# Reordering the two sums of the first down-projection slot in a fused diffusion backbone

## The chip, the cores and the metric

One core of one Trainium2 chip. The metric is the device time of one execution in microseconds. The engines named below are TensorE (PE; its weight loads are PEld), VectorE (DVE), ScalarE (ACT), GpSimd (POOL) and SyncE (SP, which issues most DMAs). Work of different engines is ordered by semaphores alone.

## What is computed

A two-layer backbone over 256 context and 256 latent tokens with 1024 features. Each layer is FFN, token mixer, FFN. The mixer of layer 0 is a state-space layer (S5) with a gated output (glu), that of layer 1 a gated DeltaNet. So there are four FFNs, f0 to f3:

```python
def swiglu(h, w13, w2):
    a, b = jnp.split(h @ w13, 2, axis=-1)
    return (jax.nn.silu(a) * b) @ w2
# D_MODEL 1024, D_FF 2816
h = ada_norm(x, norm_g[i, 0], mx[:, 0], mx[:, 1])
x = x + 0.5 * mx[:, 2] * swiglu(h, ffn_w13[i, 0], ffn_w2[i, 0])
```

The vectors `mx` (shift, scale, gate) come from the products of a conditioning vector with `mod_w`. f0, f1 and f2 are computed for all 512 tokens, f3 for the 256 latent tokens only. All is float32.

## The kernel before

**Numbers.** Every operand of a large product is split into a high part in the reduced format fp32r and the rest (low part). One tile product is three matmuls: high x high, low x high, high x low (`mm3`, L220: L223, L224 and L225). The stationary operand is a 128x128 weight tile, the moving one 512 columns of tokens (256 in f3).

**Stages.** An FFN has 22 inner tiles (2816 / 128), worked in three parts, `PARTS`, of n = 8, 8 and 6 inner tiles; "f1p2" is part 2 of FFN 1. A part has an up phase of n slots (one slot makes one inner tile of both products `a` and `b`, L242) and a down phase of four slots. A down slot takes one weight block and makes two output tiles: q = 0 in PSUM bank 4 and q = 1 in bank 5, each a sum over the part's n inner tiles. Slots alternate between two weight buffers, s = 0 and 1; a loop step i has both.

**Hidden tiles.** After an up slot ACT takes the SiLU (L636), DVE multiplies (gate, L665), POOL makes the high copy `hidh` (L722) and the low part `hidl` (L724), and increments `hid_ready`. The last of these is made while the first down slot runs. There TensorE goes through q = 0 tile by tile, waits for the last two tiles at k = n-2 and n-1 (L601), and then goes through q = 1.

**Waits of a down slot on TensorE.** `weights_in(pe, 0, ...)` and `weights_in(pe, 1, ...)` wait for the halves of the weight block, the second at the eighth tile product (`HALF // P`, L598). `x_ready[q]` (L596) says that DVE has used the bank's last sum. After q = 0 `acc_even` is incremented (L605), and in some slots `mods_turn` follows (L607, eight small transposing matmuls of L774, with which computed mod vectors are handed to DVE). After q = 1 `blk_done` is incremented (L609). `mods_step` and, in f0, `tables_pe` (L612, L613) follow the slot.

**DVE in a down slot** (`update`, L669), in fixed order: `mods_take` where `mods_turn` was issued; wait for `acc_even`; first update of `x` (`add_to_x`, L707, two instructions for 512 columns, then `x_ready[0]`); in f0 `tables_first_dve` (L680: tables for the state-space layer, bx at L1115 to L1117 and cx at L1151 to L1153, in slots set by a table); in f1p2 `mods_dve` (L682, four reductions of L786) in both slots with s = 0; wait for `blk_done`; second update (`x_ready[1]`). Between two `update`s stand the `split_lo` (L278) of the next weight block, which frees `raw` for SP's next load, and which itself follows ACT's `split_hi` (L272). The split of the weights for the first down slot stands ahead of the last gate.

**Loops.** `loop` (L527) runs a body as a hardware loop (`Fori`) or written out. On TensorE the down phases of f0 are written out (g is a number there), those of f1, f2 and f3 are loops of two steps.

Of the kernel before, what the change touches and what calls it, by code (L numbers as in the profile page):

```python
# [21 lines left out]
KT = D // P  # L22
# [71 lines left out]
def mods_where(f, p):  # L94

    g = MODS_IN.get((f, p))
    return g is not None and g >= PE_GROUPS
# [10 lines left out]
X_BEFORE = [sum(X_UPDATES[:m]) for m in range(len(NORMS) + 1)]  # L108
# [5 lines left out]
def pieces_before(m, of=("ffn", "s5", "gdn")):  # L114

    return sum(p for p, (_, _, _, k) in zip(PIECES[:m], NORMS[:m]) if k in of)
# [9 lines left out]
def program(nc, A, out):  # L126

    ctx = ExitStack()
    with ctx:
# [3 lines left out]
        def pair(name):  # L133
            return [sem(f"{name}{i}") for i in range(2)]
# [21 lines left out]
        early = ExitStack()  # L156
# [58 lines left out]
        x_ready = pair("x_ready")  # L215
# [4 lines left out]
        def mm3(pe, dst, slot, c, xh, xl, first, last):  # L220

            w_h, w_l = whi[:, slot, c:c + P], wlo[:, slot, c:c + P]
            pe.matmul(dst, w_h, xh, start=first, stop=False)  # L223
            pe.matmul(dst, w_h, xl, start=False, stop=False)  # L224
            return pe.matmul(dst, w_l, xh, start=False, stop=last)  # L225
# [10 lines left out]
        def mm3_pair_low_last(pe, dsts, slot, cs, xh, xl, low, first, last):  # L236

            for of, moving in ((whi, xh), (wlo, xh), (whi, xl)):
                if moving is xl and low:
                    pe.wait_ge(norm_done, low)  # L240
                for dst, c in zip(dsts, cs):
                    ended = pe.matmul(dst, of[:, slot, c:c + P], moving, start=first and of is whi and moving is xh, stop=last and moving is xl)  # L242
            return ended
# [19 lines left out]
        def weights_in(pe, half, s, use):  # L263

            pe.wait_ge(wlo_ready[half][s], 1 + use + 1)
# [38 lines left out]
        def halves(c0):  # L304
            return [w for w in range(2) if w * CTX >= c0]
# [221 lines left out]
        def loop(eng, n, written_out, body, first=0):  # L527

            if written_out:
                for i in range(first, n):  # L530
                    body(i)
            else:
                with eng.Fori(first, n) as i:
                    body(i)

        def mods_after(f, p):

            g = MODS_IN.get((f, p))
            return (g, PARTS[p][1] - PARTS[p][0]) if g else (None, 0)

        def ffn_pe(pe, f):
            c0, stage = NORMS[NORM_OF_FFN[f]][2], X_STAGE_OF_FFN[f]
            made = pieces_before(NORM_OF_FFN[f], ("ffn", "gdn"))
            for p, (t0, t1) in enumerate(PARTS):
                a, b, n = f"f{f}p{p}a", f"f{f}p{p}b", t1 - t0
                g, hosts = (None, 0) if mods_where(f, p) else mods_after(f, p)
                pairs = FT // 2 * f + t0 // 2

                def up_tile(i, s, k, meets_norm):
                    if k == KT // 2:  # L550
                        weights_in(pe, 1, s, BASE[a] // 2 + i)
                    low = 0
                    if meets_norm:
                        pe.wait_ge(hh_ready, pieces_before(NORM_OF_FFN[f]) + len(halves(c0)) * (k + 1))
                        low = made + len(halves(c0)) * (k + 1)
                    return mm3_pair_low_last(pe, (PS[:, s, c0:T], PS[:, 2 + s, c0:T]), s, (2 * k * P, (2 * k + 1) * P),
                                             hh[:, k, c0:T], hl[:, k, c0:T], low, k == 0, k == KT - 1)

                def up_begins(i, s):
                    if f == 0:  # L560
                        tables_room_pe(pe, BASE[a] + 2 * i + s)
                    weights_in(pe, 0, s, BASE[a] // 2 + i)
                    pe.wait_ge(gt_ready[s], 1 + pairs + i)

                def up_ends(i, s, last):
                    last.then_inc(blk_done[s], 1)
                    if g:
                        mods_step(pe, g, 2 * i + s, 7)
                    if f == 0:
                        tables_pe(pe, BASE[a] + 2 * i + s)  # L570

                def up(i):
                    for s in range(2):
                        up_begins(i, s)
                        for k in range(KT):
                            last = up_tile(i, s, k, p == 0 and s == 0 and f == 0)
                        up_ends(i, s, last)

                def up_both():
                    for s in range(2):  # L580
                        up_begins(0, s)
                    for k in range(KT // 2):
                        for s in range(2):
                            up_tile(0, s, k, s == 0)
                    for s in range(2):
                        for k in range(KT // 2, KT):
                            last = up_tile(0, s, k, s == 0)
                        up_ends(0, s, last)

                def down(i):  # L590
                    for s in range(2):
                        if f == 0:
                            tables_room_pe(pe, BASE[b] + 2 * i + s)
                        weights_in(pe, 0, s, BASE[b] // 2 + i)
                        for q in range(2):
                            pe.wait_ge(x_ready[q], 1 + X_BEFORE[stage] + KT // 2 * p + 2 * i + s)  # L596
                            for k in range(n):
                                if n * q + k == HALF // P:  # L598
                                    weights_in(pe, 1, s, BASE[b] // 2 + i)
                                if s == 0 and q == 0 and k >= n - 2:  # L600
                                    pe.wait_ge(hid_ready[k % 2], 1 + pairs + n // 2)  # L601
                                last = mm3(pe, PS[:, 4 + q, c0:T], s, (n * q + k) * P, hidh[:, k, c0:T], hidl[:, k, c0:T],
                                           k == 0, k == n - 1)
                            if q == 0:
                                last.then_inc(acc_even, 1)  # L605
                                if g and 2 * i + s == (0 if hosts == KT else 2):
                                    mods_turn(pe, g)  # L607
                            else:
                                last.then_inc(blk_done[s], 1)  # L609
                        if g and hosts + 2 * i + s < KT:  # L610
                            mods_step(pe, g, hosts + 2 * i + s, 7)
                        if f == 0:  # L612
                            tables_pe(pe, BASE[b] + 2 * i + s)  # L613

                ahead = p == 0 and f > 0
                if ahead:
                    up_both()
                loop(pe, n // 2, g, up, int(ahead))
                for s in range(2):
                    pe.wait_ge(hid_ready[s], pairs + n // 2)  # L620
                loop(pe, KT // 4, g, down)

        def ffn_act(act, f):
            c0 = NORMS[NORM_OF_FFN[f]][2]
# [125 lines left out]
        def mods_step(pe, g, k, bank):  # L750

            if k == 0 and g:
                pe.wait_ge(mod_rows, g)
            mods_landed(pe, g, k)
            weights = modw[:, k % MS, :] if g else first_group(k)
            for j in range(4):
                last = pe.matmul(PS[32 * j:32 * j + 32, bank, :], cvec[:, k, :], weights[:, 512 * j:512 * j + 512],  # L757
                                 start=k == 0, stop=k == KT - 1, tile_position=(0, 32 * j))
            last.then_inc(mod_used[k % MS], 1)
# [432 lines left out]
        def tables_room_pe(pe, j):  # L1192

            for b in range(NB5):
                for r in range(2):
                    if j == TABLE_AT[b] + 2 + 2 * r + 2:
                        pe.wait_ge(vws_ready, 2 * (2 * b + r + 1))
                if j == TABLE_AT[b] + 5:
                    pe.wait_ge(zs_ready, b + 1)
# [1497 lines left out]
```

## Time and profile before

| | |
|---|---|
| median of 3 runs | 2074.53 us (2072.89 to 2074.91) |
| profiled execution, own time | 2075.02 us |
| its span, first to last instruction | 2073.2 us |
| TensorE busy | 1971.4 us, 95% |
| DVE busy | 1473.1 us, 71% |
| ACT / POOL busy | 690.8 us, 33% / 412.7 us, 20% |
| mean granted TensorE clock | 0.978 of full |
| chain that ended last | PE 85%, DVE 8%, ACT 2%, issue 2%, POOL 1% |
| down phases of f0 | 140.5 to 191.2, 299.0 to 348.8, 429.2 to 470.1 us |
| down phases of f1 | 754.8 to 798.5, 885.4 to 929.0, 994.2 to 1032.6 us |
| down phases of f2 | from 1128.7, 1259.3 and 1368.1 us |
| down phases of f3 | from 1910.4, 1980.6 and 2039.3 us |

Times of rows are microseconds from the span's start. Busy time of an engine is the sum of its instructions' records. Matmuls overlap: the records of a 512-column one are 0.39 us long at full clock and start 0.23 us apart, so the pace is read from starts. What stands in brackets at the end of a row is the idle time of the engine before it and who ended it.

### The profile page before, as it was taken

How to read it: one execution, taken by the hardware profiler on the slowest of the kernel's cores; microseconds unless marked ns; L12 is line 12 of the kernel's file. 1: busy time of each engine (PE TensorE's matmuls, PEld its weight loads, DVE VectorE, ACT ScalarE, POOL GpSimd, SP SyncE). 2: the span in 40 equal slices, each digit the busy share in tenths (PEclk: the TensorE clock that was granted, in tenths of full speed). 3: DMA queues.
4: the chain of work that ended last, by engine and by line, in shares of the span. 5: the costliest groups of instructions: out<-in, count | busy, mean ns of one | idle time of the engine just before them, and what ended most of it. 6: DMA issues, size and time to landing. Idle time of an engine off the chain costs nothing.

```text
span 2073.2 us, 37686 instructions
## 1 busy us (share of the span) xinstructions
PE 1971.4 (95%) x15074; PEld 1677.4 (81%) x15074; DVE 1473.1 (71%) x2364; ACT 690.8 (33%) x1128; POOL 412.7 (20%) x345
## 2 busy tenths in 40 slices
PE   5999999998998999999899999998999999889997
PEld 3778778777977888888788888886889998779997
DVE  6968778758646976848998585357677777755555
ACT  4222222133344312222232122225555555434332
POOL 0220110134731221202413021140000000013113
PEclk9999999999999999999999999998999999989998
DMA  8465675657633454534535453222011111024553
GB/s 333 163 235 200 204 236 185 213 180 276 254 113 130 162 182 143 192 132 159 186 122 182 142 196 108 96 86 86 27 49 53 43 43 56 30 82 156 180 177 96
DMA packets 85637, 305.11 MB, mean 147 GB/s; under 512 B 9856, under 2 KB 21632, under 8 KB 76032
## 3 DMA queue, kind: packets, MB, share of 16 engines
q1 hardware_dynamic: 80896, 285.41, 40.0%
q0 software_dynamic: 2304, 9.44, 1.1%
q10 hardware_dynamic: 2304, 8.39, 1.0%
q8 instruction: 96, 1.57, 0.3%
q14 instruction: 37, 0.30, 0.0%
HBM read 275.94 MB, written 27.26 MB: 146 GB/s over the span
## 4 chain that ended last, share of the span: by engine, by line
PE 85%; DVE 8%; ACT 2%; issue 2%; DMA 1%; POOL 1%; SPq 1%; DVEq 0%; ACTq 0%; POOLq 0%
PE PS L242 38%; PE PS L223 6%; PE PS L224 6%; PE PS L225 6%; PE PS L1797 6%; PE PS L1784 6%; PE PS L232 4%; PE PS L1379 1%; DVE wlo L278 1%; PE PS L757 1%; DMA et<-in_mod_w 1%; PE PS L1211 1%; PE PS L1185 1%; POOL hidl L724 1%; PE PS L1995 1%
## 5 line engine op out<-in xcount | busy, mean ns | idle before, releaser
L278 DVE TENSOR_TENSOR wlo<-raw,whi 128x1024 fp32r<-128x1024 f32 x313 | 454.8, 1492 | 68.4 <-ACT whi L272 66.7
L242 PE MATMUL PS<-hh,whi 128*128 128x512 f32 (+1 forms) x1408 | 402.7, 368 | 9.1 <-ACT hh L381 7.9
L242 PE MATMUL PS<-hh,wlo 128*128 128x512 f32 (+1 forms) x1408 | 399.5, 365 | 0.0
L272 ACT ACTIVATE whi<-raw 128x1024 fp32r<-128x1024 f32 x300 | 301.5, 1052 | 294.0 <-PE PS L225 253.2
L242 PE MATMUL PS<-hl,whi 128*128 128x512 f32 (+1 forms) x1408 | 399.1, 365 | 0.0
L242 PEld LDWEIGHTS PS<-hh,whi 128*128 128x128 f32 x1408 | 254.1, 191 | 56.6 <-issue 12.0
L242 PEld LDWEIGHTS PS<-hh,wlo 128*128 128x128 f32 x1408 | 255.6, 191 | 42.2
L242 PEld LDWEIGHTS PS<-hl,whi 128*128 128x128 f32 x1408 | 255.3, 191 | 42.4 <-DVE hl L493 0.6
L223 PE MATMUL PS<-hidh,whi 128*128 128x512 f32 (+1 forms) x704 | 258.4, 367 | 9.7 <-POOL hidl L724 7.0
L224 PE MATMUL PS<-hidl,whi 128*128 128x512 f32 (+1 forms) x704 | 256.1, 364 | 0.0
L225 PE MATMUL PS<-hidh,wlo 128*128 128x512 f32 (+1 forms) x704 | 256.1, 364 | 0.0
L722 POOL CAST hidh<-gt 128x512 f32 (+2 forms) x88 | 64.8, 737 | 934.6 <-DVE gt L665 934.6
L636 ACT ACTIVATE gt<-PS 128x512 f32<-128x512 f32 (+1 forms) x88 | 47.9, 545 | 607.3 <-PE PS L242 607.3
L786 DVE CUSTOM_DVE_ANT_0 junk<-modw,cb,modb 128x1024 f32<-128x1024 f32 x160 | 219.0, 1369 | 6.7 <-ACT cb L631 2.4
L707 DVE SCALAR_TENSOR_TENSOR x<-PS,hg,x 128x256 f32<-128x256 f32 (+1 forms) x176 | 77.9, 478 | 145.1 <-PE PS L225 142.1
L724 POOL TENSOR_TENSOR hidl<-gt,hidh 128x512 f32 (+2 forms) x88 | 161.3, 1832 | 12.6 <-POOL hidh L722 10.8
L223 PEld LDWEIGHTS PS<-hidh,whi 128*128 128x128 f32 x704 | 133.3, 189 | 34.7 <-POOL hidl L724 9.3
L665 DVE TENSOR_TENSOR gt<-gt,PS 128x512 f32<-128x512 f32 (+1 forms) x88 | 54.6, 621 | 135.8 <-ACT gt L636 131.6
L225 PEld LDWEIGHTS PS<-hidh,wlo 128*128 128x128 f32 x704 | 133.3, 189 | 21.0
L224 PEld LDWEIGHTS PS<-hidl,whi 128*128 128x128 f32 x704 | 133.2, 189 | 19.9
L2426 POOL TENSOR_TENSOR X<-BT,consts 128x256 f32<-128x256 f32 x16 | 13.5, 843 | 343.8 <-DVE BT L2267 343.8
L1797 PE MATMUL PS<-hh,whi 128*128 128x512 f32 (+1 forms) x256 | 72.7, 366 | 2.6 <-DVE hl L493 2.5
(353 smaller groups left out, 2770.6 us busy)
## 6 DMA issues: line engine op xcount, KB each, us to landing
modw<-in_mod_w SPq DMA_DIRECT2D x66, 1024.0 KB, 5.0
raw<-in_w_gdn SPq DMA_DIRECT2D x32, 512.0 KB, 3.9
cxd<-cx POOLq DMA_DIRECT2D x16, 576.0 KB, 6.8
cxS<-cxd SPq DMA_DIRECT2D x8, 1152.0 KB, 6.0
raw<-in_w_f0p0a SPq DMA_DIRECT2D x16, 512.0 KB, 7.8
vwd<-vws ACTq DMA_DIRECT2D x16, 512.0 KB, 6.9
raw<-in_w_f0p1a SPq DMA_DIRECT2D x16, 512.0 KB, 5.4
raw<-in_w_glu SPq DMA_DIRECT2D x16, 512.0 KB, 4.3
```

The source lines that it names most:

```text
L223: pe.matmul(dst, w_h, xh, start=first, stop=False)
L224: pe.matmul(dst, w_h, xl, start=False, stop=False)
L225: return pe.matmul(dst, w_l, xh, start=False, stop=last)
L232: ended = pe.matmul(dst, of[:, slot, c:c + P], moving, start=first and part_ == 0, stop=last and part_ == 2)
L242: ended = pe.matmul(dst, of[:, slot, c:c + P], moving, start=first and of is whi and moving is xh, stop=last and moving is xl)
L272: act.activation(whi[:, s, c], raw[:, s, c], ACT.Copy).then_inc(whi_ready[half][s], 1)
L278: dve.tensor_tensor(wlo[:, s, c], raw[:, s, c], whi[:, s, c].bitcast(F32), ALU.subtract)\
L707: last = dve.scalar_tensor_tensor(out=xv, in0=pv, scalar=hg[:, layer, n, bass.ds(dt, 1), w:w + 1].rearrange("p a b -> p (a b)"), in1=xv, o ...
L724: pool.tensor_tensor(hidl[:, bass.ds(2 * i + s, 1), c0:T], gt[:, s:s + 1, c0:T], hidh[:, bass.ds(2 * i + s, 1), c0:T].bitcast(F32), ALU.su ...
L786: dve.tensor_tensor_reduce(out=junk[:, :], in0=modw[:, k % MS, D * j:D * j + D], in1=cb[:, w, :], scale=1.0, scalar=modb[:, layer, a:a + 1 ...
L1784: return pe.matmul(dst, lhsT, rhs, start=True, stop=True, tile_position=(SUB * at_row, SUB * at_col))
L1797: last = pe.matmul(PS[:, 2 * s + i, 0:T - c0], (whi, whi, wlo)[part_][:, s, (2 * k + i) * P:(2 * k + i + 1) * P], (hh, hl, hh)[part_][:, k ...
```

## The change

In the first down slot of each part, (i, s) = (0, 0), TensorE takes all inner tiles but the last two for bank 4, then the same for bank 5, then the last two for bank 4, then the last two for bank 5. All other slots keep their order. So that the first slot can differ, the down phases of all parts are written out on TensorE. `acc_even`, `mods_turn` and `blk_done` stay behind the last matmul of their bank.

```diff
@@ -592,15 +592,24 @@
                         weights_in(pe, 0, s, BASE[b] // 2 + i)
-                        for q in range(2):
-                            pe.wait_ge(x_ready[q], 1 + X_BEFORE[stage] + KT // 2 * p + 2 * i + s)
-                            for k in range(n):
+                        late = [n - 2, n - 1]
+                        early = [k for k in range(n) if k not in late]
+                        if (i, s) == (0, 0):
+                            parts_ = [(0, early), (1, early), (0, late), (1, late)]
+                        else:
+                            parts_ = [(0, early + late), (1, early + late)]
+                        for q, ks in parts_:
+                            if ks[0] == 0:
+                                pe.wait_ge(x_ready[q], 1 + X_BEFORE[stage] + KT // 2 * p + 2 * i + s)
+                            for k in ks:
                                 if n * q + k == HALF // P:
                                     weights_in(pe, 1, s, BASE[b] // 2 + i)
                                 if s == 0 and q == 0 and k >= n - 2:
                                     pe.wait_ge(hid_ready[k % 2], 1 + pairs + n // 2)
                                 last = mm3(pe, PS[:, 4 + q, c0:T], s, (n * q + k) * P, hidh[:, k, c0:T], hidl[:, k, c0:T],
                                            k == 0, k == n - 1)
+                            if ks[-1] != n - 1:
+                                continue
                             if q == 0:
                                 last.then_inc(acc_even, 1)
@@ -618,7 +627,7 @@
-                loop(pe, KT // 4, g, down)
+                loop(pe, KT // 4, True, down)
```

## Rows read from the trace of the kernel before

**Rows 1.** The page: busy time, share of the span and instructions of TensorE.
```profile
PE 1971.4 (95%) x15074; PEld 1677.4 (81%) x15074; DVE 1473.1 (71%) x2364; ACT 690.8 (33%) x1128; POOL 412.7 (20%) x345
```
**Rows 2.** The waits of TensorE: us in total, times, longest.
```profile
PE PS L223 <- POOL hidl L724: 7.0, 7, 1.5
```
**Rows 3.** Timeline of f0p0's down phase: start, duration, engine, line, operation.
```profile
140.87 0.39 PE L224 MATMUL PS<-hidl,whi 128*128 128x512 f32 x1
...
145.21 0.39 PE L225 MATMUL PS<-hidh,wlo 128*128 128x512 f32 x1
146.22 0.50 PE L223 MATMUL PS<-hidh,whi 128*128 128x512 f32 x1 [0.62 <-POOL hidl L724]
...
146.79 0.39 PE L225 MATMUL PS<-hidh,wlo 128*128 128x512 f32 x1
...
148.44 0.88 DVE L707 SCALAR_TENSOR_TENSOR x<-PS,hg,x 128x256 f32<-128x256 f32 x2
...
154.50 0.40 PE L224 MATMUL PS<-hidl,whi 128*128 128x512 f32 x1
...
158.57 0.88 DVE L707 SCALAR_TENSOR_TENSOR x<-PS,hg,x 128x256 f32<-128x256 f32 x2 [0.15 <-DVE cx L1153]
```
**Rows 4.** Timeline of f0p1's down phase, first slots.
```profile
299.31 0.39 PE L224 MATMUL PS<-hidl,whi 128*128 128x512 f32 x1
...
305.94 0.87 DVE L707 SCALAR_TENSOR_TENSOR x<-PS,hg,x 128x256 f32<-128x256 f32 x2
...
312.06 0.39 PE L224 MATMUL PS<-hidl,whi 128*128 128x512 f32 x1
...
316.11 0.88 DVE L707 SCALAR_TENSOR_TENSOR x<-PS,hg,x 128x256 f32<-128x256 f32 x2
```
**Rows 5.** Timeline of f1p2's down phase, first slots.
```profile
994.23 0.39 PE L223 MATMUL PS<-hidh,whi 128*128 128x512 f32 x1
...
998.79 0.50 PE L223 MATMUL PS<-hidh,whi 128*128 128x512 f32 x1 [1.00 <-POOL hidl L724]
999.79 0.88 DVE L707 SCALAR_TENSOR_TENSOR x<-PS,hg,x 128x256 f32<-128x256 f32 x2
...
1006.65 0.88 DVE L707 SCALAR_TENSOR_TENSOR x<-PS,hg,x 128x256 f32<-128x256 f32 x2
```
**Rows 6.** Idle and clock: timeline rows, then windows (us, engines' busy, PEclk, DMA share, GB/s).
```profile
495.38 2.08 PE L1341 MATMUL PS<-U,whi 128*64 128x64 f32 x64 [2.00 <-DVEq L1475]
...
1025.68 0.87 DVE L707 SCALAR_TENSOR_TENSOR x<-PS,hg,x 128x256 f32<-128x256 f32 x2
...
1026.61 0.50 PE L223 MATMUL PS<-hidh,whi 128*128 128x512 f32 x1 [2.30 <-DVE x L707]
...
1032.21 0.40 PE L225 MATMUL PS<-hidh,wlo 128*128 128x512 f32 x1
...
39.97 1.20 PE L242 MATMUL PS<-hh,whi 128*128 128x512 f32 x2 [3.95 <-ACT hh L381]
...
40.00:44.00 4.00, 4.00 (x10) 3.14 (x11) 4.00 (x9) 2.35 (x6) 0.00 (x0) 0.50 1.02 423
1028.00:1031.00 3.00, 3.00 (x8) 2.33 (x8) 2.97 (x4) 0.00 (x0) 2.71 (x2) 0.50 0.96 380
```
**Rows 7.** The other down phases: timeline rows, then two windows (f1p0, f3p0).
```profile
434.19 0.50 PE L223 MATMUL PS<-hidh,whi 128*128 128x512 f32 x1 [1.27 <-POOL hidl L724]
...
1913.88 0.39 PE L223 MATMUL PS<-hidh,whi 128*128 128x256 f32 x1 [0.85 <-POOL hidl L724]
...
1917.68 0.48 DVE L707 SCALAR_TENSOR_TENSOR x<-PS,hg,x 128x256 f32 x1 [2.37 <-PE PS L225]
...
2042.70 0.39 PE L223 MATMUL PS<-hidh,whi 128*128 128x256 f32 x1 [1.46 <-POOL hidl L724]
...
754.80:798.50 43.70, 43.70 (x194) 36.18 (x194) 17.96 (x26) 8.53 (x9) 2.68 (x2) 1.00 0.42 144
1910.30:1934.40 24.10, 23.25 (x194) 23.05 (x194) 13.43 (x16) 8.41 (x9) 2.09 (x2) 1.00 0.55 179
```

## What I predicted before seeing the result

> **What bounds the kernel now.** I read the busy shares first: TensorE computes for 95% of the span [rows 1], so a change counts only where TensorE waits or where it moves TensorE. Then the list of waits, to see what the change can take away: TensorE waits for the low parts of the hidden tiles (`hidl`, POOL) 7 times, 7.0 us in all [rows 2]. Then the timeline of each of the twelve down phases, and in it two things: where the first sum stops for `hidl`, and what VectorE (DVE) does between the two updates of `x`. Last the granted clock around idle stretches.
>
> In the text "f0p0" is FFN 0, part 0; a slot is one weight block, 2n tile products into bank 4 and bank 5, three matmuls each, so 48 matmuls (n = 8) or 36 (n = 6). Matmuls of a slot are counted from 1.
>
> **What it removes.** The first down slot now runs both sums as far as tile n-2 before it needs the last two. TensorE comes to them after 36 (n = 8) or 24 (n = 6) matmuls instead of 18 or 12. At 0.228 us each (145.21 less 140.87 over 19 matmuls, [rows 3]) that is 8.2 or 5.5 us after the slot's start; the waits now end 5.7 us (f0p0), about 5 us (f0p2, 434.19 in [rows 7] against a start at 429.2) and 4.6 us (f1p2, [rows 5]) after it. So the wait vanishes wherever 512 columns run. The matmuls of 256 columns (f3) run at 0.120 us (23.25 us for 194, [rows 7]): 4.3 us for n = 8 against 3.5 us, gone; 2.9 us for n = 6 against 3.4 us, so 0.5 us stays.
>
> Gain per part, measured at the slot's end. An idle of x costs x + 0.16 (the record is 0.39 us long, the pace 0.23), and 0.1 more at the restart (146.22 to 146.79 is 0.57 us for two intervals, [rows 3]). f0p0: 0.62 gives 0.88. f0p2: 1.27 gives 1.54. f1p2: 1.00 gives 1.26, and f2p2 has the same wait [rows 5]. f3p0 and its like f3p1: 0.85 + 0.16 + 0.1 = 1.11. f3p2: the sum of 21 matmuls behind the wait becomes one of 12, 9 x 0.12 = 1.08. f0p1, f1p0, f1p1, f2p0, f2p1 have no wait to lose: f1p0's phase is 43.70 us of 43.70 busy [rows 7]. Together 0.88 + 1.54 + 2.52 + 2.22 + 1.08 = 8.24 us.
>
> **What it moves.** Bank 4 is complete only 6 matmuls before the slot's end: as matmul 42 instead of 24 (n = 8), 30 instead of 18 (n = 6). On it hang acc_even, in f0p0 and f0p1 the eight transposes of `mods_turn`, and then, in DVE's fixed order: first update of `x`, whatever stands between the updates, second update, split_lo of the next weights. The second update frees bank 5 for the second slot (`x_ready[1]`).
>
> In most parts nothing stands between the updates. The first update takes 0.88 us, starts some 0.43 us after the last matmul's issue, and wakes TensorE 0.06 us after its end (1025.68 + 0.87 to 1026.61, [rows 6]): 1.37 us, while the second slot begins 7 x 0.2264 = 1.58 us after that matmul (f1's pace: 43.70 us for 193 starts, [rows 7]). It fits by 0.2 us. In f3 the second slot begins 7 x 0.12 = 0.84 us after it, but the update (0.48 us) starts up to 0.58 us later (matmul 48 at 1913.88 + 0.23 + 25 x 0.12 = 1917.11, its update at 1917.68, [rows 7]), 1.12 us in all: a new stall of 0.28 + 0.1 us in f3p0 and f3p1. That leaves 0.73 each: the gain falls by 0.76 to 7.48 us.
>
> Three parts have work between the updates.
> - f0p0: `tables_first_dve` (bx, then cx). Bank 4's last matmul was at 146.79 and the first update at 148.44, 1.65 us later through the transposes. Now matmul 42 is at 140.87 + 40 x 0.2284 = 150.01, so the update is at 151.66, 3.22 us later. The chain behind it has no idle time, so the second update goes from 158.57 to 161.79, and TensorE may start bank 5 at 161.79 + 0.87 + 0.06 = 162.72. In the second slot this is matmul 25, before at 154.50 + 23 x 0.2284 = 159.75 [rows 3], and 158.87 with the 0.88 gained. Stall 3.85 us; net against before +2.97, in place of -0.88.
> - f0p1: the first update moves by 18 x 0.2284 = 4.11 us, the second from 316.11 to 320.22, wake 321.15. Matmul 25 of the second slot was due at 312.06 + 23 x 0.2284 = 317.31 and still is [rows 4]. Stall 3.84 us, net +3.84.
> - f1p2: four mods reductions (`mods_dve`) from 999.79 to 1006.65, 6.86 us [rows 5]. Matmul 30 is now at 994.23 + 29 x 0.2264 = 1000.80, update at 1001.23 (+1.44), second update 1008.09, wake 1009.02. Matmul 19 of the second slot comes at 994.23 + 54 x 0.2264 = 1006.46. Stall 2.56 us; before it ran at 998.79 + 0.33 + 38 x 0.2264 = 1007.72, so net +1.30 in place of -1.26. The second stall of this phase, 2.30 us [rows 6], hangs by ACT's and DVE's splits on the end of the second slot, so it moves along and hides nothing.
>
> **What the clock adds.** After the idle of 2.30 us the granted clock fell from 1.00 to 0.50 (1.2 instead of 2.4 GHz): eight matmuls in the 3.00 us from 1028, and the 18 matmuls from 1026.61 to 1032.21 took 5.60 us instead of 17 x 0.2264 = 3.85, 1.75 us lost, restart included [rows 6]. After an idle of 2.00 us (ending at 495.38) the next stretch shows 64 matmuls in 2.08 us, which is full pace, and the three 1.0 to 1.3 us waits cost no clock. Behind the idle of 3.95 us that ended at 39.97, 4.00 us ran at 0.50 [rows 6], 2.0 us lost. The new stalls leave idles of 3.7, 3.7 and 2.4 us, beyond the 2.30 that sufficed. I take 2.0, 2.0 and 1.75; bounds 0.1 each (restart alone) and 2.2 each. The Trainium skill, "TensorE: Matmul & The Clock Gate", section "Back-to-back issue gap", gives 512 / 1.2 and 512 / 2.4 + 2.5 ns; as an estimate from it a matmul loses 0.211 us at the low clock, where the rows show 3.00 / 8 less 0.227, some 0.15 to 0.2. The sum would not move by 0.3 us.
>
> **The rest.** Nine parts' down phases become straight code on TensorE. The loop's edges show no gap now (43.70 of 43.70 busy), so there is nothing to gain. Fetching more code could cost: f0's phases are written out already and pace at 0.2284 against 0.2264, with a busier DVE beside them; if all of that were code, 1056 matmuls of f1 and f2 x 0.0020 = 2.1 us. I take 0, since the 4.34 us in [rows 3] run beside tables on DVE that f1 and f2 don't have. No DMA issue moves on SP; POOL's two cx stores of f0p0 and f0p1 start 3 to 4 us later, and nobody waits for them before the next phase. The earlier wait for the second half of the weights costs nothing: DVE splits them ahead of the gate that `hidl` needs.
>
> **Sum.** f0p0 2.97 + 2.0, f0p1 3.84 + 2.0, f1p2 1.30 + 1.75: +13.86. Less f0p2 1.54, f2p2 1.26, f3 0.73 + 0.73 + 1.08: -5.34. +8.5 us on the profiled execution's own 2075.02, 2083.5; on the median 2074.53, **2083.0 us**, 0.41% slower.
>
> **Rivals.**
> - The stalls come but the clock holds: three times 0.1 instead of 5.75, +3.0 us, 2077.6. For it speaks the idle of 2.00 us at full pace and that TensorE is dense before each stall; against it the drop after 2.30 us, equally dense before. The same page says in "Loop structure matters more than you think" that DVE's copy out of PSUM does not break the array's warmth; by that rule this rival holds. The trace disagrees at 1026.61, where the wait was for just such an update.
> - The other side, faster: the second sum of the next slot does not meet the late update, since DVE would finish tables and reductions in time. It needs the shift of the second update to stay below the slack that stands there now, 0.3 us in f0p0 (159.75 against 158.57 + 0.93) and f0p1, while I work out 3.2 and 4.1. Then 7.5 us are gained, 2067.0. Only a hole in DVE's chain that I read as full would do it.
> - Dearer: the code written out, or a low clock that lasts through the rest of the sum. 2.1 us for the first, and 0.2 to 0.45 more for each of the three stalls (2.2 instead of 2.0 and 1.75), 0.85 in all: 2083 + 3 = 2086; were every one of nine phases to lose 0.5 us at its entry, 2087.5.
>
> **How the numbers follow.** Forecast 0.72, clock holds 0.12, faster 0.06, dearer 0.10. The forecast's own range is 2080.5 to 2085.5 (one drop less, all bounds up). The range goes down to the second case and half way into the last: 2077.0 to 2086.5. A measurement of this kernel tells about 0.2%, 4.1 us, from no change. Faster 0.06; within 0.2% (to 2078.7) 0.13; slower 0.81.
>
> **What would show it.** Right: TensorE waits for `hidl` only in f3p2, some 0.4 us; three new waits of L223 for DVE's L707, 3.7, 3.7 and 2.4 us, at the middle of the second down slot of f0p0, f0p1 and f1p2, each with a clock of 0.50 behind it; the wait of 2.30 us in f1p2 unchanged. Wrong: no such wait (the DVE step falls), waits with a clock of 1.00 (the clock step falls), or gaps put down to issue at the starts of the written-out phases (the code step falls).

## The result and the profile after

The changed kernel takes 2079.86 us (median of 5 runs, 2078.25 to 2081.79) against 2073.45 us (5 runs, 2072.89 to 2074.91): ratio 1.0027, 95% interval 1.0016 to 1.0039. It is slower by 6.4 us by the medians; forecast was 8.5 us. The measured median lies inside the whole range of the prediction (2077.0 to 2086.5) and 0.6 us below the range of its forecast case (2080.5 to 2085.5). The profiled executions' own times stand at 2079.86 and 2075.02, 4.8 us apart. (In this kernel's listing the lines behind the change are 9 higher: DVE's update of `x` is L716, the reductions L795, POOL's `hidl` L733.)

The page of the kernel after gives the busy times of the engines. TensorE is busy 6.1 us longer than before; DVE and POOL differ from before by 2.4 us.

```profile
span 2078.0 us, 37623 instructions
PE 1977.5 (95%) x15074; PEld 1683.6 (81%) x15074; DVE 1475.5 (71%) x2364; ACT 690.8 (33%) x1128; POOL 410.3 (20%) x345
```

The waits of TensorE, after (us in total, times, longest): the line of [rows 2], L223 for POOL's `hidl`, is gone. The waits for DVE's update, 2.5 us in all before, are now longer than both kinds together were.

```profile
PE PS L223 <- DVE x L716: 11.7, 7, 3.7
```

The timeline of f0p0 after, beside [rows 3]. Bank 4's chain starts at 151.00, the second update at 161.13 has DVE's tables right ahead of it, and TensorE starts bank 5 of the second slot 0.06 us after it ends, having idled 3.69 us.

```profile
151.00 0.88 DVE L716 SCALAR_TENSOR_TENSOR x<-PS,hg,x 128x256 f32<-128x256 f32 x2
...
161.13 0.87 DVE L716 SCALAR_TENSOR_TENSOR x<-PS,hg,x 128x256 f32<-128x256 f32 x2 [0.15 <-DVE cx L1162]
...
162.06 0.70 PE L223 MATMUL PS<-hidh,whi 128*128 128x512 f32 x1 [3.69 <-DVE x L716]
```

The same in f0p1 (beside [rows 4]) and f1p2 (beside [rows 5]):

```profile
314.06 0.87 DVE L716 SCALAR_TENSOR_TENSOR x<-PS,hg,x 128x256 f32<-128x256 f32 x2
...
324.23 0.87 DVE L716 SCALAR_TENSOR_TENSOR x<-PS,hg,x 128x256 f32<-128x256 f32 x2
325.16 0.50 PE L223 MATMUL PS<-hidh,whi 128*128 128x512 f32 x1 [3.69 <-DVE x L716]
...
1011.49 0.88 DVE L716 SCALAR_TENSOR_TENSOR x<-PS,hg,x 128x256 f32<-128x256 f32 x2 [1.39 <-PE PS L225]
...
1018.36 0.88 DVE L716 SCALAR_TENSOR_TENSOR x<-PS,hg,x 128x256 f32<-128x256 f32 x2
...
1019.29 0.80 PE L223 MATMUL PS<-hidh,whi 128*128 128x512 f32 x1 [2.38 <-DVE x L716]
```

Behind each of the three idles the granted clock (third number from the right) is at 0.50, the low one of the two levels. The windows are from the kernel after, in the columns of [rows 6]:

```profile
163.00:165.00 2.00, 2.00 (x6) 1.61 (x5) 1.75 (x5) 0.00 (x0) 0.00 (x0) 0.50 0.43 173
326.00:329.00 3.00, 3.00 (x9) 2.32 (x8) 2.75 (x6) 0.00 (x0) 0.00 (x0) 0.50 0.32 129
1020.00:1022.00 2.00, 2.00 (x6) 1.54 (x5) 2.00 (x2) 0.00 (x0) 1.92 (x2) 0.50 0.22 55
```

The remaining place is the end of f1p2, where before the wait of 2.30 us stood [rows 6]. After, it is 1.25 us, and the 18 matmuls behind it take 1042.54 less 1038.55 = 3.99 us instead of 5.60:

```profile
1037.63 0.87 DVE L716 SCALAR_TENSOR_TENSOR x<-PS,hg,x 128x256 f32<-128x256 f32 x2
...
1038.55 0.50 PE L223 MATMUL PS<-hidh,whi 128*128 128x512 f32 x1 [1.25 <-DVE x L716]
...
1042.54 0.39 PE L225 MATMUL PS<-hidh,wlo 128*128 128x512 f32 x1
```

A phase's time is taken here from the first matmul of the down phase to the first of what follows it. The table has the time after less the time before:

| part | forecast | measured in the profiles |
|---|---|---|
| f0p0 | +4.97 | +4.66 |
| f0p1 | +5.84 | +5.61 |
| f0p2 | -1.54 | -1.56 |
| f1p2 | +3.05 | +0.06 |
| f2p2 | -1.26 | -1.27 |
| f3p0, f3p1 | -0.73 each | -0.67 each |
| f3p2 | -1.08 | -1.35 |
| f1p0, f1p1, f2p0, f2p1 | 0 | within 0.06 |
| sum | +8.5 | +4.8 |

Outside these phases the profiles differ too: +0.7 us in the S5 stage, +1.4 in the first up phase of f1, +1.0 and then -1.3 around the norm behind f1, -0.5 in the DeltaNet, -0.6 ahead of the first down phase and -0.8 behind the last start of a matmul. They cancel to within 0.1 us. In the S5 stage, for instance, both kernels idle 2.00 us at the same place. Before, 64 matmuls followed in 2.08 us (the row at 495.38 in [rows 6]); after, the same 64 took 3.57 us, at the low clock:

```profile
503.62 3.57 PE L1350 MATMUL PS<-U,whi 128*64 128x64 f32 x64 [2.00 <-DVEq L1484]
...
503.62:506.80 3.18, 3.18 (x60) 3.18 (x62) 3.18 (x6) 0.45 (x1) 3.10 (x3) 0.50 0.42 167
```

So the row by which the prediction held an idle of 2.00 us to be free was one of two outcomes.

### The profile page after: what moved, and what is told of

It reads as the page before. It is cut to its first block, busy times and chain, and to the rows that moved or that the text cites. A ratio compares the mean times of both kernels' runs of the same rounds, so it can differ in the third digit from the quotient of the medians.

```text
span 2078.0 us, 37623 instructions
## 1 busy us (share of the span) xinstructions
PE 1977.5 (95%) x15074; PEld 1683.6 (81%) x15074; DVE 1475.5 (71%) x2364; ACT 690.8 (33%) x1128; POOL 410.3 (20%) x345
## 4 chain that ended last, share of the span: by engine, by line
PE 88%; DVE 7%; ACT 1%; issue 1%; DMA 1%; DVEq 0%; SPq 0%; POOL 0%; ACTq 0%
PE PS L242 40%; PE PS L223 6%; PE PS L224 6%; PE PS L225 6%; PE PS L1793 6%; PE PS L1806 6%; PE PS L232 4%; PE PS L1388 1%; PE PS L766 1%; DVE wlo L278 1%; PE PS L1220 1%; PE PS L1350 1%; DMA et<-in_mod_w 1%; PE PS L1370 1%; PE PS L1194 1%
## 5 line engine op out<-in xcount | busy, mean ns | idle before, releaser
L223 PE MATMUL PS<-hidh,whi 128*128 128x512 f32 (+1 forms) x704 | 259.7, 369 | 11.8 <-DVE x L716 11.7
L795 DVE CUSTOM_DVE_ANT_0 junk<-modw,cb,modb 128x1024 f32<-128x1024 f32 x160 | 218.0, 1362 | 6.7 <-ACT cb L640 2.4
L716 DVE SCALAR_TENSOR_TENSOR x<-PS,hg,x 128x256 f32<-128x256 f32 (+1 forms) x176 | 78.0, 478 | 142.0 <-PE PS L225 139.2
L733 POOL TENSOR_TENSOR hidl<-gt,hidh 128x512 f32 (+2 forms) x88 | 161.4, 1834 | 12.6 <-POOL hidh L731 10.8
L223 PEld LDWEIGHTS PS<-hidh,whi 128*128 128x128 f32 x704 | 133.9, 190 | 36.8 <-DVE x L716 12.7
```

The costliest lines, as they stand in the source:

```text
L716: last = dve.scalar_tensor_tensor(out=xv, in0=pv, scalar=hg[:, layer, n, bass.ds(dt, 1), w:w + 1].rearrange("p a b -> p (a b)"), in1=xv, o ...
L733: pool.tensor_tensor(hidl[:, bass.ds(2 * i + s, 1), c0:T], gt[:, s:s + 1, c0:T], hidh[:, bass.ds(2 * i + s, 1), c0:T].bitcast(F32), ALU.su ...
L795: dve.tensor_tensor_reduce(out=junk[:, :], in0=modw[:, k % MS, D * j:D * j + D], in1=cb[:, w, :], scale=1.0, scalar=modb[:, layer, a:a + 1 ...
```

## The experiments

The theory: the cost is DVE's late second update where work stands between its two updates, plus the clock that falls in the idle; the gain is the removed wait for `hidl` elsewhere; the code written out is free. The rivals are that the written-out code costs, that the clock plays no part, and that the order itself is dear.

### Only the code written out

```diff
-                        if (i, s) == (0, 0):
+                        if (i, s) == (0, 0) and False:
```

> The down phases written out on TensorE, with the order of before in every slot (the change's other half alone). Theory (the stalls behind DVE's late update are the cost, the code is free): within 1 us of before, waits for hidl as before (seven, 7.0 us), one wait of 2.30 us for the update in f1p2. Rival (more code costs): +2.1 us (1056 matmuls of f1 and f2 times 0.0020), or new idle put down to issue at the phases' starts.

Measured 2073.91 us (11 runs) against 2073.23 (23 runs), ratio 1.0002 (0.9993 to 1.0011). The down phases of f1, f2 and f3 are as long as before within 0.1 us each, and no idle is put down to issue at their starts. The rival of +2.1 us lies at 1.0010, inside the interval's end, but the phases' own lengths exclude it. The waits for `hidl` stand as before, except in f0p0, where there is none and the phase is 0.9 us shorter. Of the eight kernels of this section with f0p0 in the old order, five lack that wait and three have it, so it isn't the edits that decide whether the 0.62 us of [rows 3] appears.

### The new order in f0p0 and f0p1 alone

```diff
+                        if (i, s) == (0, 0) and (f, p) in ((0, 0), (0, 1)):
```

> All down phases written out, the new order in the first slots of f0p0 and f0p1 alone, where the tables stand between DVE's two updates. Theory: two idles of 3.7 us at the middle of the second slots, each with a clock of 0.50 behind it, +4.97 +5.84 = +10.8 us against before; the profile of the changed kernel had +4.66 and +5.61, so +10.3. If the clock held: +7.0. If the changed kernel's cost lay in its other parts: below +3.

Measured 2086.22 us (5 runs) against 2073.23, ratio 1.0062 (1.0049 to 1.0075), +13.0 us. In the profile both idles are 3.70 us and the phases +5.59 and +6.37, 11.96 in all. So these two parts alone cost more than the whole change; the clock-holds rival (+7.0) is out.

Their code is that of the changed kernel, and the idles are as long, yet f0p0 costs 0.93 us more here and f0p1 0.76. The low clock lasted longer. The row and a window of this kernel:

```profile
162.69 0.80 PE L223 MATMUL PS<-hidh,whi 128*128 128x512 f32 x1 [3.70 <-DVE x L716]
...
166.00:167.90 1.90, 1.90 (x6) 1.51 (x5) 1.90 (x4) 0.00 (x0) 0.00 (x0) 0.50 0.37 97
```

The same window of the changed kernel, whose idle ended at 162.06:

```profile
166.00:167.90 1.90, 1.90 (x10) 1.55 (x9) 1.90 (x4) 0.00 (x0) 0.00 (x0) 1.00 0.69 153
```

### The new order in f1p2 alone

```diff
+                        if (i, s) == (0, 0) and (f, p) == (1, 2):
```

> All down phases written out, the new order in the first slot of f1p2 alone. By the prediction's step (the second wait of the phase moves along unchanged): +3.05 us. By what the changed kernel's profile showed (the second wait shrinks from 2.30 to 1.25 us and the clock stays up behind it, 1.75 us not lost there): +0.1 us for the phase. An early stall of 2.4 us at the second slot's middle with a low clock in either case.

Measured 2075.08 us (12 runs) against 2073.23, ratio 1.0006 (0.9997 to 1.0016). The phase is +0.13 us in the profile, with idles of 2.39 and 1.25 us, as in the changed kernel. The step of the prediction that moved the second wait along unchanged is wrong here too, and so not by the chance of one execution.

### The new order where nothing stands between the updates

```diff
+                        if (i, s) == (0, 0) and (f, p) in ((0, 2), (2, 2), (3, 0), (3, 1), (3, 2)):
```

> All down phases written out, the new order only in f0p2, f2p2, f3p0, f3p1 and f3p2, where a wait for hidl stands and nothing stands between DVE's two updates of the first slot. Theory: the gains of these five parts alone, 1.54 + 1.26 + 0.73 + 0.73 + 1.08 = 5.3 us, so faster than before by 5.3 us (0.26%). If the freed time is lost again in later waits or to the clock's phase: within 2 us of before.

Measured 2064.93 us (5 runs, 2063.99 to 2066.65) against 2073.23, ratio 0.9957 (0.9944 to 0.9970): 0.43% faster than before. The five phases give 1.60 + 1.24 + 0.67 + 0.67 + 1.36 = 5.5 us, the forecast's gain. By the medians another 2.8 us come on top. In the profile two more places are shorter than before, and this kernel leaves both in the old order: f0p0 by 0.9 us (there is no wait for `hidl`) and the end of f1p2 by 1.6 us. At the latter, after the same idle as in the kernel with only the code written out, the clock stayed up.

The row and window of the kernel with only the code written out:

```profile
1029.08 0.50 PE L223 MATMUL PS<-hidh,whi 128*128 128x512 f32 x1 [2.35 <-DVE x L716]
...
1030.50:1033.00 2.50, 2.50 (x7) 1.93 (x6) 2.47 (x4) 0.00 (x0) 2.42 (x2) 0.50 0.97 360
```

The same place in this kernel:

```profile
1026.99 0.50 PE L223 MATMUL PS<-hidh,whi 128*128 128x512 f32 x1 [2.35 <-DVE x L716]
...
1027.00:1032.00 5.00, 4.92 (x34) 3.60 (x34) 4.97 (x6) 0.60 (x1) 4.11 (x2) 1.00 0.87 312
```

Idle 2.35 us in both, clock 0.50 in one and 1.00 in the other: at this length an idle may or may not cost the 1.6 us.

### The same, with the other phases as loops again

```diff
-                loop(pe, KT // 4, True, down)
+                loop(pe, KT // 4, g or f == 3 or (f, p) == (2, 2), down)
```

> The new order only in f0p2, f2p2, f3p0, f3p1 and f3p2, and the down phases of f1p0, f1p1, f1p2, f2p0 and f2p1 again as loops, so that nothing of the change is left where it brings nothing. Theory: the five parts gain 5.5 us as in the profile of the kernel with all phases written out (1.60, 1.24, 0.67, 0.67, 1.36); what that kernel gained beyond, 2.8 us, came in stretches that the change doesn't touch, through the clock, and need not come again: 2065 to 2070. Rival: the excess belongs to the change and comes again, 2065, whatever the loops are.

Measured 2066.43 us (5 runs) against 2075.10 (9 runs), ratio 0.9955 (0.9942 to 0.9969). The five phases give 1.56 + 1.29 + 0.68 + 0.67 + 1.36 = 5.6 us. The ratio again says some 9 us: 5.6 us would be 0.9973, outside the intervals of both kernels. So an excess of some 3 us came twice, which speaks for the rival. But its places in the profile are again f0p0 (0.9 us) and the end of f1p2 (1.6 us, no fall of the clock), and the kernel with four tiles behind in f0p1, below, shows both though it has the old order in all five parts. These two places alone are thus no proof that the excess belongs to the change. With one profiled execution of each kernel, why the medians are that low stays open.

### How far the update moves: four and six tiles behind, in f0p1

These are two kernels; the first has `n - 4` in the line below, the second `n - 6`.

```diff
-                        late = [n - 2, n - 1]
+                        late = list(range(n - 4, n))
...
+                        if (i, s) == (0, 0) and (f, p) == (0, 1):
```

> All down phases written out, the new order in the first slot of f0p1 alone, with the last four inner tiles of each sum behind instead of two. Bank 4 ends as matmul 36 instead of 42, so DVE's chain moves by 12 x 0.2284 = 2.74 us instead of 4.11. Theory: TensorE waits 2.74 - 0.27 = 2.47 us at the middle of the second slot (an idle of 2.3 us), part +2.5 us if the clock holds, +4.2 if it falls as it did after 2.30 us. Rival (the cost doesn't come from the shift of the first update): the same as with two tiles behind, idle 3.7 us, +5.6.

> The same with the last six inner tiles behind: bank 4 ends as matmul 30, the chain moves by 1.37 us. Theory: a wait of 1.10 us (idle 0.94), the clock stays at 1.00, part +1.2 us. Rival: as with two tiles behind, idle 3.7 us, +5.6.

With four behind, the row and the window after it:

```profile
318.33 0.50 PE L223 MATMUL PS<-hidh,whi 128*128 128x512 f32 x1 [2.34 <-DVE x L716]
...
319.00:323.00 4.00, 4.00 (x12) 3.11 (x11) 3.72 (x8) 0.00 (x0) 0.00 (x0) 0.57 0.34 125
```

With six behind:

```profile
317.65 0.50 PE L223 MATMUL PS<-hidh,whi 128*128 128x512 f32 x1 [0.98 <-DVE x L716]
...
317.60:322.00 4.40, 4.35 (x19) 3.61 (x20) 4.05 (x9) 0.00 (x0) 0.00 (x0) 1.00 0.33 134
```

The phase is +4.25 and +1.29 us (forecast 4.2 and 1.2), with the clock down in the one and up in the other; with two behind it was +5.61. Overall ratios: 1.0023 (1.0011 to 1.0034) and 1.0004 (0.9994 to 1.0013). Each six matmuls by which bank 4 completes earlier shorten the idle by 1.35 us (3.69, 2.34, 0.98).

The kernel with four behind also bears on the end of f1p2, a phase that it leaves in the old order. There the clock stayed at 1.00 and the phase is 1.61 us shorter than before:

```profile
1033.57 0.50 PE L223 MATMUL PS<-hidh,whi 128*128 128x512 f32 x1 [2.30 <-DVE x L716]
...
1033.60:1037.60 4.00, 4.00 (x18) 3.27 (x18) 3.97 (x5) 0.00 (x0) 3.92 (x2) 1.00 0.89 330
```

### The tables behind the second update, in f0p1

```diff
+                    behind = (f, p) == (0, 1) and (i, s) == (0, 0)
+                    if not behind:
+                        between()
                     dve.wait_ge(blk_done[s], 1 + BASE[b] // 2 + i + 1)
                     add_to_x(dve, layer, n_, 4 * i + 2 * s + 1, c0, 5, None).then_inc(x_ready[1], 1)
+                    if behind:
+                        between()
```

> All down phases written out, the new order in the first slot of f0p1 alone, and there DVE makes its tables behind its second update instead of between the two. Theory: no wait at the middle of the second slot. DVE's whole work comes next: second update at about 311.1, tables 9.3 us, the coefficients, the split of the third slot's weights and the next first update end near 326.8, and the third slot starts before at 325.2, so TensorE waits 1.5 to 1.7 us at the start of the third slot, the clock stays up, part +1.8 us instead of +5.6. Rival (the new order itself is dear there, not the place of the tables): +5.6 again.

`between()` holds the tables and reductions. DVE and TensorE of that kernel (its L723 is the update of `x`):

```profile
308.43 0.87 DVE L723 SCALAR_TENSOR_TENSOR x<-PS,hg,x 128x256 f32<-128x256 f32 x2
309.54 0.88 DVE L723 SCALAR_TENSOR_TENSOR x<-PS,hg,x 128x256 f32<-128x256 f32 x2 [0.24 <-PE PS L225]
...
322.13 2.36 DVE L278 TENSOR_TENSOR wlo<-raw,whi 128x1024 fp32r<-128x1024 f32 x2
324.41 0.87 DVE L723 SCALAR_TENSOR_TENSOR x<-PS,hg,x 128x256 f32<-128x256 f32 x2
...
325.43 0.47 PE L223 MATMUL PS<-hidh,whi 128*128 128x512 f32 x1 [1.75 <-DVE x L723]
```

The updates are 1.1 us apart instead of 10.2, the wait at the second slot's middle is gone, and the next one stands where it was expected, 1.75 us at the third slot's start. The phase is +1.78 us. The order itself is not dear; DVE has 9.3 us of tables in this slot and no room to begin them late. The whole: ratio 1.0018 (1.0006 to 1.0030).

### POOL's squares made small

```diff
-                pool.tensor_tensor(dst[:, c0:T], xv, xv, ALU.mult).then_inc(sum_step, 1)
+                c1 = c0 + 8 if m == 3 else T
...
+                pool.tensor_tensor(dst[:, c0:c1], xv, xv, ALU.mult).then_inc(sum_step, 1)
...
-                pool.tensor_tensor(std[:, c0:T], std[:, c0:T], rstd[:, c0:T], ALU.add).then_inc(sum_step, 1)
+                c1 = c0 + 8 if m == 3 else T
+                pool.tensor_tensor(std[:, c0:c1], std[:, c0:c1], rstd[:, c0:c1], ALU.add).then_inc(sum_step, 1)
...
-                        if (i, s) == (0, 0):
+                        if (i, s) == (0, 0) and False:
```

> The order of before in all slots, down phases written out, and POOL's squares and sums behind FFN 1 made over 8 columns instead of 512 (so the norm behind FFN 1 is not the reference's). If POOL's work beside DVE is what stretches DVE's splits (4.25 us for two in f1p2) and reductions (1.9 to 2.2 instead of 1.28), both fall to 2.4 and 1.28 us, some 3.7 us less between the updates, and the wait of 2.35 us in the last down slot of f1p2 is gone or below 0.3. Rival (DMA traffic or the weights' arrival stretches them): durations and wait as before.

This asks why the second wait of f1p2 shrank. The kernel leaves out most of the squares and sums behind FFN 1, so it computes another norm. It ran once (2066.57 us), and only its durations are used.

Before (in the old order), DVE's two splits behind the second slot and POOL beside them:

```profile
1012.11 0.88 DVE L707 SCALAR_TENSOR_TENSOR x<-PS,hg,x 128x256 f32<-128x256 f32 x2 [0.68 <-PE PS L225]
1013.18 1.29 POOL L445 TENSOR_TENSOR std<-std,rstd 128x512 f32<-128x512 f32 x1
1013.29 4.25 DVE L278 TENSOR_TENSOR wlo<-raw,whi 128x1024 fp32r<-128x1024 f32 x2 [0.31 <-ACT whi L272]
1014.99 1.47 POOL L436 TENSOR_TENSOR rstd<-x 128x512 f32 x1 [0.51 <-POOL std L445]
```

After the change:

```profile
1024.89 1.30 POOL L445 TENSOR_TENSOR std<-std,rstd 128x512 f32<-128x512 f32 x1
1025.10 0.87 DVE L716 SCALAR_TENSOR_TENSOR x<-PS,hg,x 128x256 f32<-128x256 f32 x2 [1.97 <-PE PS L225]
1026.28 3.21 DVE L278 TENSOR_TENSOR wlo<-raw,whi 128x1024 fp32r<-128x1024 f32 x2 [0.31 <-ACT whi L272]
```

With small squares:

```profile
1013.33 0.88 DVE L718 SCALAR_TENSOR_TENSOR x<-PS,hg,x 128x256 f32<-128x256 f32 x2 [2.13 <-PE PS L225]
1014.51 2.37 DVE L278 TENSOR_TENSOR wlo<-raw,whi 128x1024 fp32r<-128x1024 f32 x2 [0.31 <-ACT whi L272]
...
1023.82 0.87 DVE L718 SCALAR_TENSOR_TENSOR x<-PS,hg,x 128x256 f32<-128x256 f32 x2
```

The pair of splits takes 4.25, 3.21 and 2.37 us, the way from second update to second update 13.57, 12.53 and 10.49. All the reductions are back at 1.28 us, the wait of 2.30 us is gone and the phase 4.3 us shorter (2.5 of it the wait, the rest mostly the clock that stayed up). So it is POOL's work that stretches DVE's beside it. It stretches by less than the time that both run: 4.25 less 2.37 is 1.88 us, while the two engines overlap for some 3.6 us. That in the changed kernel the overlap is smaller is read from the rows: POOL's sum ends at 1026.19, ahead of the split, while before it ran beside it from 1013.29 to 1014.47. The chain is 1.04 us shorter. That POOL was further on because DVE idled 1.97 us ahead of its update is argued only.

## Why the prediction was right, point by point

**The wait that was removed.** Right in place and size: f0p2, f2p2 and f3p0/f3p1 within 0.06 us. In f3p2 I let matmul 25 wait for the last tile. It is tile n-1 alone, so matmul 28, that needs it; tile n-2 was ready. The gain was 1.35 instead of 1.08, and no wait of 0.4 us for `hidl` remained.

**The step that decided the sign.** The move of `acc_even`, and with it DVE's chain, was worked out to 3.2, 4.1 and 1.4 us. The idles came at 3.69, 3.69 and 2.38 us against 3.7, 3.7 and 2.4. f0p1 moved with the number of tiles behind (idles 3.7, 2.34, 0.98), and placing the tables elsewhere moved the wait; both are shown, by an edit of one thing each.

**The clock.** Right that it falls behind all three. Its price was 1.69 (4.66 less 2.97) and 1.77 us (5.61 less 3.84) in the changed kernel, but 2.62 and 2.53 (5.59 and 6.37 less the same) in the kernel with these two parts alone. So the 2.0 that I took lies between, and my upper bound of 2.2 was too low. The price follows the length of the low stretch: a matmul in it starts 0.426 us after the one before, in these rows of the kernel before.

```profile
1028.11 0.63 PE L225 MATMUL PS<-hidh,wlo 128*128 128x512 f32 x1
...
1030.24 0.63 PE L224 MATMUL PS<-hidl,whi 128*128 128x512 f32 x1
```

These are five intervals in 2.13 us, so a matmul loses 0.20 us. The 3.00 / 8 of the prediction is misread, since the window also counts the matmuls that its ends cut.

The rival in which the clock holds is out for the long idles. For an idle of 2.3 to 2.4 us it is not. The clock fell behind eight of the eleven in all kernels: at the end of f1p2 in the kernel before and four others, behind the early stall of f1p2 (twice), and in f0p1 with four tiles behind. It did not fall in three kernels at the end of f1p2, behind 2.30, 2.35 and 2.35 us. Nor is 2.00 us safe, as the prediction had it: behind the idle in the S5 stage the clock held in the kernel before and fell in the changed one. By the Trainium skill, "TensorE: Matmul & The Clock Gate", section "Loop structure matters more than you think", DVE's copy out of PSUM doesn't break the array's warmth where the next matmuls follow immediately. The prediction took this for a sum that has to wait for such a copy, which the scheme there doesn't show; here, behind waits of 3.69 us for DVE's update, the clock fell to 0.50.

**The term that was mis-sized.** f1p2: +3.05 forecast, +0.06 measured. I said its second stall "moves along and hides nothing". It shrank by 1.05 us, since POOL's sums overlapped DVE's splits less, and an idle of 1.25 us instead of 2.30 left the clock up, 1.61 us saved behind it. Together 2.7 of the 3.0 us. I had taken DVE's durations from rows made beside POOL's work and moved them as if they were fixed. These 3 us are most of what stands between the forecast of +8.5 and the profile's +4.8.

**Where it was luck.** The parts of the profile give little more than half of the forecast; the medians, +6.4, come closer to it, and no step of the prediction says why. The length of the low stretches alone moves the same two parts by 1.7 us from one kernel to another, a good part of the change's own size. So the sign and the places are shown, and the closeness of the total is partly chance.

**The rest.** The written-out code is free, as taken. The rival in which the kernel is faster (DVE done in time) needed a hole in DVE's chain; there was none.

## What to carry to other kernels

Before two accumulations are interleaved to cover a late operand, look at who waits for the first one to finish. The change kept TensorE busy for 1 us and delayed a consumer that had 9.3 us of other work queued between its two outputs and 0.3 us of slack. Apply such an order only where the consumer is idle: with the five parts that gain, the kernel is 0.43% faster than before, of which their own phases account for 5.5 us or 0.27%; with all twelve it is 0.27% slower.

## What I had not expected of the hardware

An idle of 2.35 us of TensorE was followed by a clock of 0.50 in one kernel and of 1.00 in another, at the same place of the program, and so was one of 2.00 us. In the down phases idles up to 1.75 us were never followed by the low clock, and those of 3.69 and 3.70 us always were (four). Behind those four the same code lost from 1.7 to 2.6 us. And POOL's elementwise work over 512 columns stretched a pair of DVE's splits from 2.37 to as much as 4.25 us and a reduction from 1.28 to 2.19 us.
